# A two-block transformer kernel: the second expert table becomes the stationary operand, and the end of the kernel keeps features on the partitions

## The reference, cut to what matters

```
h = h + peer(rms_norm(h, ffn_norm_gain), w_pq, sub_k1, sub_k2, expert_u, expert_v)
gate = sigmoid(rms_norm(h, ple_norm_gain) @ w_ple_gate)
h = h + gate * (p @ w_ple_proj)

def peer(xn, ...):             # 8 heads; 128 x 128 = 16384 experts
    # top 16 of 128 keys twice per head, top 16 of the 256 pairs -> eidx, gates (128 per token)
    act = gelu(einsum('tkd,td->tk', expert_u[eidx], xn))
    return einsum('tk,tkd->td', act * gates, expert_v[eidx])
```

## Time and profile before

| | us |
|---|---|
| median of 3 runs | 3196.07 |
| the profiled execution | 3203.04 |
| its span | 3201.3 |
| TensorE busy in it | 3064.3 (96%) |
| TensorE weight loads | 2653.1 (83%) |
| VectorE busy | 1886.7 (59%) |
| ScalarE busy | 1458.6 (46%) |
| DMA | 665.24 MB, mean 208 GB/s |

### The profile page before, as it was taken

One profiled execution on the slowest core, in us unless ns is written; L12 is line 12 of the kernel. 1 busy time (PEld: TensorE's weight loads), 2 busy tenths in 40 slices (PEclk: granted clock), 3 DMA queues, 4 the chain that ended last, 5 costly groups with the idle time before them and its releaser, 6 DMA issues. The chain is left out here.

```text
span 3201.3 us, 39991 instructions
## 1 busy us (share of the span) xinstructions
PE 3064.3 (96%) x15672; PEld 2653.1 (83%) x15672; DVE 1886.7 (59%) x2657; ACT 1458.6 (46%) x2137; POOL 159.9 (5%) x282
## 2 busy tenths in 40 slices
PE   8997689999998999999999999999999999999998
PEld 7996677888887887977789899889998888888876
DVE  4445355444444545464558987998755655655554
ACT  4333444444443444354444466347644444444443
POOL 2002100000000000140000100110000000000000
PEclk9996699999999999999999999999999999999999
DMA  7552045555554554545567888888787666777653
GB/s 247 188 188 68 0 148 172 192 185 194 185 188 158 192 196 145 173 142 178 192 211 247 281 304 305 293 278 294 257 276 241 240 231 242 242 248 248 216 194 131
DMA packets 219049, 665.24 MB, mean 208 GB/s; under 512 B 11705, under 2 KB 87513, under 8 KB 169488
## 3 DMA queue, kind: packets, MB, share of 16 engines
q1 hardware_dynamic: 208592, 607.36, 56.6%
q0 software_dynamic: 5440, 35.80, 3.2%
q10 hardware_dynamic: 4864, 19.99, 1.7%
HBM read 623.25 MB, written 37.77 MB: 206 GB/s over the span
## 5 line engine op out<-in xcount | busy, mean ns | idle before, releaser
L195 DVE TENSOR_TENSOR weights_lo<-weights,weights_hi 128x1024 fp32r<-128x1024 f32 (+4 forms) x1080 | 1227.5, 1178 | 974.8 <-ACT weights_hi L188 973.3
L188 ACT ACTIVATE weights_hi<-weights 128x1024 fp32r<-128x1024 f32 (+4 forms) x1080 | 1046.8, 1018 | 1508.8 <-PE banks L444 1121.4
L2185 PE MATMUL banks<-peer_features,weights_hi 128*128 128x448 f32 (+1 forms) x2304 | 743.7, 378 | 18.7 <-DVE weights_lo L195 18.6
L442 PE MATMUL banks<-weights_hi,features_hi 128*128 128x512 f32 (+3 forms) x1728 | 651.5, 377 | 11.4 <-DVE weights_lo L195 11.3
L444 PE MATMUL banks<-weights_hi,features_lo 128*128 128x512 f32 (+3 forms) x1728 | 649.3, 376 | 0.0
L443 PE MATMUL banks<-weights_lo,features_hi 128*128 128x512 f32 (+3 forms) x1728 | 649.1, 376 | 0.0
L2186 PE MATMUL banks<-peer_features,weights_lo 128*128 128x224 f32 (+1 forms) x2304 | 615.1, 267 | 0.0
L2185 PEld LDWEIGHTS banks<-peer_features,weights_hi 128*128 128x128 f32 x2304 | 431.9, 187 | 68.7 <-DVE weights_lo L195 27.9
L2186 PEld LDWEIGHTS banks<-peer_features,weights_lo 128*128 128x128 f32 x2304 | 438.6, 190 | 0.0
L442 PE MATMUL banks<-weights_hi,applied_hi 128*128 128x512 f32 x1024 | 398.5, 389 | 1.1 <-DVE peer_scores L2362 1.1
L444 PE MATMUL banks<-weights_hi,applied_lo 128*128 128x512 f32 x1024 | 398.4, 389 | 0.0
(11 more groups left out here) (377 smaller groups left out, 2101.8 us busy)
## 6 DMA issues: line engine op xcount, KB each, us to landing
weights<-in_expert_u SPq DMA_DIRECT2D x128, 1024.0 KB, 5.8
weights<-in_expert_v SPq DMA_DIRECT2D x128, 1024.0 KB, 5.0
weights<-in_w_ffn_gate SPq DMA_DIRECT2D x44, 1024.0 KB, 5.2
weights<-in_w_ffn_up SPq DMA_DIRECT2D x44, 1024.0 KB, 5.2
weights<-in_w_ffn_down SPq DMA_DIRECT2D x44, 1024.0 KB, 5.0
weights<-in_w_in SPq DMA_DIRECT2D x48, 900.0 KB, 4.7
weights<-in_w_out SPq DMA_DIRECT2D x32, 1024.0 KB, 5.2
weights<-in_w_in SPq DMA_DIRECT2D x24, 704.0 KB, 4.4
```

What stands on the lines that cost most here:

```text
L188: act.activation(hi[:, k, n], raw[:, k, n], ACT.Copy).then_inc(self.hi_ready, 1 + skip)
L195: last = dve.tensor_tensor(lo[:, k, n], raw[:, k, n], hi[:, k, n].bitcast(F32), ALU.subtract)
L442: pe.matmul(out, xh, wh, start=first, stop=False)
L2185: pe.matmul(self.bank(n % 3, 2 * (T - lo)), wh[:, k, :], F[:, k, :, lo:T], start=(k == 0), stop=False)
```

## The change

It has five parts.

1. **Second table.** The stationary operand is now a 128 x 128 tile of the table, and the moving one the weights of 224 tokens: 48 matmuls of 224 columns to a step in place of 24 of 512. The sum lies in PSUM with features on the partitions. At the first step eight matmuls of a zero tile with 512 columns clear the banks.
2. **The 32 tokens.** Their chosen rows of `expert_v` are gathered too, 32 more gathers of 1 MB; VectorE sums them, each scaled, at 64 places (`ADD`) in steps 158 to 261, and 16 small fp32 matmuls with a 0/1 matrix at step 266 add them into the banks. The gate matrix is no longer built for them: steps 126 to 129 of `HOT` and a set of transposes are gone. Scores and gates in DRAM are 224 tokens wide.
3. **The first table's row products** (`SUM`) move from steps 34 to 118 to steps 56 to 73 and 108 to 153, one at each step.
4. **The residual** is turned in place to features on the partitions: 8 times 4 transposes at steps 76, 79, ..., 97 (`BACK`), each with one ScalarE copy of 512 elements.
5. **The end** is part of the same block and the same ring: 16 further steps with `w_ple_gate_2` as the stationary operand, 768 matmuls of 256 columns. The transposes after the second table are gone; norm statistics, sigmoid, product, sum and store (10 stores of 128 or 256 KB) work on features by tokens. `project` in the earlier stage makes the projection in that layout (the same columns in twice as many matmuls). The output is stored transposed, and the host turns it.

```diff
@@ project (earlier stage)
-                for t in range(NT):
+                for m in range(4):
                     for k in range(2):
-                        last = pe.matmul(self.bank(banks + t), pT[:, k, tok(t)], wproj[c // 2][:, c % 2, k, :],
-                                         start=(k == 0), stop=(k == 1))
+                        last = pe.matmul(self.bank(banks + m // 2, T, m % 2 * T), wproj[c // 2][:, c % 2, k, m * P:(m + 1) * P],
+                                         pT[:, k, :], start=(k == 0), stop=(k == 1))
@@ constants of peer
-        SC, RET, TURN = 18, (22, 74), (55, 107, 122)
...
+        SC, RET, TURN = 18, (22, 74), (55, 107)
         ROWS, BUFS = 32, 3
-        HOT = [(58 + i, 0, ROWS // 8 + i) for i in range(16 - ROWS // 8)] + [(110 + i, 1, i) for i in range(16)]\
-            + [(126 + i, 0, i) for i in range(ROWS // 8)]
-        SUM = [34 + 4 * k // 3 for k in range(2 * ROWS)]
+        HOT = [(58 + i, 0, ROWS // 8 + i) for i in range(16 - ROWS // 8)] + [(110 + i, 1, i) for i in range(16)]
+        SUM = [56, 57, *range(58, 74), *range(108, 154)]
         DOTS = SUM[-1] + 1
+        free = [s for s in range(DOTS + 4, 262) if s % 8 != 2]
+        ADD = [free[k * len(free) // (2 * ROWS)] for k in range(2 * ROWS)]
+        GATHERED, BACK = NKEYS - 6, [76 + 3 * j for j in range(KD // 2)]
@@ tensor, first table
+                        if n in BACK:
+                            j = BACK.index(n)
+                            pe.wait_ge(choice_read, 1)
+                            if j > 0:
+                                pe.wait_ge(*x_back(j))
+                            for i in range(2):
+                                for t in range(NT):
+                                    last = pe.transpose(self.bank(5, P, i * T + t * P), chunk(t, 2 * j + i), self.ident[:, :])
+                            last.then_inc(self.turned.sem, 1)
@@ tensor, second table
+                        if e == GATHERED:
+                            pe.wait_ge(row_summed, 4 * ROWS)
+                            for c in range(KD):
+                                pe.matmul(self.bank(c // 2, ROWS, c % 2 * T), row_sum[:, c * P:(c + 1) * P], sel[:, :],
+                                          start=False, stop=False)
                         wh, wl = ring.hi[:, half, :], ring.lo[:, half, :]
-                        for t in ((1, 0) if e == 0 else (0, 1)):
...
-                            for c in range(4):
-                                cols, tok = slice(c * BANK, (c + 1) * BANK), slice(t * P, (t + 1) * P)
-                                last = self.passes(pe, self.bank(4 * t + c), a_hi[:, q % 2, e % 2, tok], a_lo[:, q % 2, e % 2, tok],
-                                                   wh[:, cols], wl[:, cols], e == 0, e == NKEYS - 1)
...
+                        gh, gl = a_hi[:, q % 2, e % 2, :], a_lo[:, q % 2, e % 2, :]
+                        for c in (range(KD) if e > 0 else [*range(6, KD), *range(6)]):
...
+                            out, cols = self.bank(c // 2, DENSE, c % 2 * T + ROWS), slice(c * P, (c + 1) * P)
+                            if e == 0 and c % 2 == 0:
+                                pe.matmul(self.bank(c // 2), zero[:, :], wh[:, 0:BANK], start=True, stop=False)
+                            pe.matmul(out, wh[:, cols], gh, start=False, stop=False)
+                            pe.matmul(out, wl[:, cols], gh, start=False, stop=False)
+                            last = pe.matmul(out, wh[:, cols], gl, start=False, stop=(e == NKEYS - 1 and c % 2 == 1))
+                            if e == NKEYS - 1 and c % 2 == 1 and c < KD - 1:
                                 last.then_inc(applied, 1)
@@ tensor, the 16 steps of the end
+                    for s in range(KD):
+                        b, piece = s // 4, s % 4
...
+                        ring.wait(pe, i, j, half)
...
+                        for c in range(4):
+                            if piece == 0 and b < 2:
+                                pe.wait_ge(added, 4 * b + c + 1)
+                            if piece == 0 and b >= 2:
+                                pe.wait_ge(gate_left, 2 * (b - 2) + c // 2 + 1)
+                            for k in range(4):
+                                kk = 4 * piece + k
+                                if b == c == 0 and k % 2 == 0:
+                                    pe.wait_ge(*f_lo(kk // 2 + 1))
+                                out, cols = self.bank(4 * (b % 2) + c, T), slice(c * P, (c + 1) * P)
+                                pe.matmul(out, wh[:, k, cols], F[:, kk, 0, :], start=(kk == 0), stop=False)
+                                pe.matmul(out, wl[:, k, cols], F[:, kk, 0, :], start=False, stop=False)
+                                last = pe.matmul(out, wh[:, k, cols], F[:, kk, 1, :], start=False, stop=(kk == KD - 1))
@@ vector, gathered rows of the second table
+                            if c == 0:
+                                last = dve.tensor_scalar(to, row, weight, None, ALU.mult)
+                            else:
+                                last = dve.scalar_tensor_tensor(out=to, in0=row, scalar=weight, in1=to, op0=ALU.mult, op1=ALU.add)
+                            last.then_inc(row_summed, 1)
@@ vector, the end: add(j), feature_lo(j), scale(n), out(n)
+                        dve.tensor_tensor(XT[:, j], self.bank(j).rearrange("p (i t) -> p i t", t=T), XT[:, j], ALU.add)\
+                            .then_inc(added, 1)
...
+                        dve.tensor_tensor(gate_of(n), gate_banks(b, c, w), R[:, :].unsqueeze(1).to_broadcast([P, w, T]),
+                                          ALU.mult).then_inc(gate_left, 1)
...
+                        ch(dve.tensor_tensor(gate_of(n), gate_of(n), proj[:, 4 * b + c:4 * b + c + w, :], ALU.mult))
+                        dve.tensor_tensor(chunks(b, c, w), chunks(b, c, w), gate_of(n), ALU.add).then_inc(out_ready, 1)
```

More of the change, by code:

```diff
@@ L2160, in _ @@
                     self.rstd_of_tiles(pool, D)
-                    for c in range(ROWS):
-                        if c % 8 == 0:
+                    for c in range(2 * ROWS):
+                        if c % 8 == 0 and c < ROWS:
                             pool.wait_ge(listed, c // 8 + 1)
@@ L2190, in _ @@
                             for t in range(NT):
-                                last = pe.matmul(self.bank(3, P, t * P), self.ones[:, :], S[:, 0, 0, t * P:(t + 1) * P],
+                                last = pe.matmul(self.bank(3, P, t * P), self.ones[:, :], S_flat[:, t * P:(t + 1) * P],
                                                  start=True, stop=True)
@@ L2247, in _ @@
                                 last.then_inc(applied, 1)
                         last.then_inc(ring.used, 1)
+                    for s in range(KD):
+                        b, piece = s // 4, s % 4
+                        i, j, half = at(END + s)
+                        ring.wait(pe, i, j, half)
+                        wh, wl = [ring.piece(w, half, ple_tiles) for w in (ring.hi, ring.lo)]
+                        for c in range(4):
[11 more added lines that the diff above has]
+                                last = pe.matmul(out, wh[:, k, cols], F[:, kk, 1, :], start=False, stop=(kk == KD - 1))
+                            if b == 3 and piece == 3 and c < 3:
+                                last.then_inc(applied, 1)
+                        last.then_inc(ring.used, 1)
+                        if s == ROWSUM:
+                            pe.wait_ge(*x_squared(KD // 2 + 1))
+                            for t in range(NT):
+                                last = pe.matmul(self.bank(0, 1, T + t), total[:, 0, t * P:(t + 1) * P], self.ones[:, 0:1],
+                                                 start=True, stop=True)
+                            last.then_inc(self.squares.sem, 1)
+                        if s == SPREAD:
+                            pe.wait_ge(diag, 2)
+                            for t in range(NT):
+                                last = pe.matmul(self.bank(1, P, T + t * P), self.ones[:, :], diagonal[:, t * P:(t + 1) * P],
+                                                 start=True, stop=True)
+                            last.then_inc(spread, 1)
@@ new lines, in feature_lo @@
+                    def feature_lo(j):
+                        dve.wait_ge(*f_hi(j + 1))
+                        for i in range(2):
+                            hi, lo = [f[:, 2 * j + i, :] for f in F_ple]
+                            last = dve.scalar_tensor_tensor(out=lo, in0=XT[:, j, i], scalar=ple_gains[2 * j + i],
+                                                            in1=hi.bitcast(F32), op0=ALU.mult, op1=ALU.subtract)
+                        last.then_inc(self.turned_read["dve"].sem, 1)
@@ L2463, in peer @@
+                    for n in range(6, len(groups)):
+                        scale(n)
+                        if n > 6:
+                            out(n - 1)
+                    out(len(groups) - 1)
```

(1 more changed line is left out.)

333 lines of the change are left out of this document (210 added, 123 removed).

## The result

The kernel after takes 3149.34 us (median of 4 runs, 3149.23 to 3149.43), beside 3198.65 for the kernel before on the same chip (4 runs, 3193.03 to 3201.77): ratio 0.9848, 95% interval 0.9831 to 0.9865, so faster by 1.5%. The forecast was 3145 with 3112 to 3175 around it. In five more runs on another chip the ratio was 0.9845 (0.9832 to 0.9859). The profiled execution took 3149.38, its span is 3147.6 where it was 3201.3: 53.7 us less.

A forecast was written before the change was run, and what follows sets the result against it. The matmuls themselves were taken as the bound, with TensorE stalls behind VectorE in two first-table stretches; −10 − 31 − 9 + 8.5 − 9.5 = −51 us from a median of 3196.07 gave 3145, range 3112 to 3175.

The forecast's parts named there:

- The five terms of the sum: Second table −10, first table −31, gap before the gate product −9, gate product +8.5, after its last matmul −9.5 us.
- the +1 for late products at steps 133 and 146: First table: at these steps L2418 meets a row product, which was to cost 1 us.
- 687.3: Second table's forecast length in us: 682.0 for its matmuls, 1.8 for clearing, 3.5 for 16 fp32 matmuls; 696.4 before.
- The gap: Between the second table's last matmul and the gate product's first: 1 us in place of 10.2, −9 us.
- the low end of my two and not the middle: Gate product's price per 256-column matmul: low end 0.1201 us, high end 0.1266, middle 0.1233 taken, giving 94.7 us.
- the fixed 0.0134 taken from 512: Time in us a matmul carries beside its columns: 512 columns at 2.4 GHz are 0.2133 of the 0.2267 measured.
- the remainder of a pair of unlike matmuls: Gate product's high end: a pair of 512 and 256 columns, 0.3533 us, less 0.2267 leaves 0.1266 for 256 columns.
- The tail's chain: After the last matmul: scaling, sigmoid, product, sum over 256 elements, then a store; 5 us in place of 14.5, −9.5.
- the 3.9 worked out: VectorE's work in us beside the second table in one step of 5.3 us, taken as covered.
- R1: Steps 126 to 143: moved work stalls its new place through DMA limits, +12 us, time 3157 to 3165; chance 0.12.
- R2: Second table: the load hides, a 224-column matmul costs 0.1067 us or less, time 3119; chance 0.13.
- R3: Second table: handover comes on top of the load, 0.1266 us a matmul, +86 us, whole kernel 3241; chance 0.06.

The follow-up runs named there:

- the run with short products: Kernel before, each of the first table's 64 row products 128 elements wide instead of 1024, place and order unchanged: 3171.5 us, ratio 0.9916.

## Why the prediction was right

The bound was read rightly. The five terms of the sum all have the sign forecast, and all but one are within some 2 us of their size; that one, and the size of the stall inside another, came from rows that were misread. The median came out 4 us above the forecast: the change gave 49.3 us instead of 51, and the median of before was 3198.65 where the forecast started from 3196.07.

*Parts 2 to 4, first table, −31 against −31.5: the mechanism is right, the closeness is partly luck.* The prediction counted 23 and 32 tiles in the two stretches, put the loss at 32 us and took 29 of it back. The stall was 26 (the run with short products). The count is of whole tiles that VectorE finished, and a tile is 5 us. The matmuls of the same two stretches of the kernel before, 1755 to 1884 and 1978 to 2157, give parts of tiles too:

```profile
L2185 PE MATMUL banks<-peer_features,weights_hi 128*128 128x448 f32 x377 | 120.7, 377 | 7.2 <-DVE weights_lo L195 7.2
...
L2185 PE MATMUL banks<-peer_features,weights_hi 128*128 128x448 f32 x527 | 168.6, 377 | 9.2 <-DVE weights_lo L195 9.2
```

377 and 527 pairs at 0.3133 are 118.1 and 165.1 us, so 10.9 + 13.9 = 25 us were lost there, and 26 over steps 34 to 107. By steps the rest is this: −7.1 over steps 126 to 143, where four one-hot steps are gone (448 records of these matmuls where there were 512; not tried alone); −1.2 over steps 108 to 125, of which 0.5 is a wait of L2228 on L2330; −1.1 for a wait of L442 on L2362 ahead of the second table, which the forecast had set down to part 1; and +3.5 for the transposes of the residual (+4.0 by the run without them). With the −25.9 that is −31.8. So 3 us too many for the stall were made good by small terms that the sum did not have here, and by the +1 for late products at steps 133 and 146, which did not come: there is no wait of TensorE there.

*Part 1, second table, −10 against −4.6: the mis-sized term.* The mechanism was right, a load of 128 columns as the floor, and is now shown from both sides: 687.96 us with 128 columns, 688.00 with 224, and 0.1186 a matmul with 256. Two sizes were off. The pace is 0.1117, not 0.111: 6144 × 0.0007 = 4.3 us, and 0.001 us in such a price is 6. The price was in the trace, and its reading was off. The prediction divided the whole length of a row by its matmuls. The loads of the same L787 in the kernel before, from the middle of the run on:

```profile
381.51 3.32 PEld L787 LDWEIGHTS banks<-sgu_v,sgu_w_turned 128*128 128x128 f32 x29
```

A load of them is recorded with 0.19, so they are (3.32 − 0.19) / 28 = 0.1118 apart. The first distance between matmuls of that run is 0.06, since the first load lay ahead of it, and pulls the mean down to the 0.110 that was read. The 16 transposes do stand 0.109 apart in steady state; 0.111 was a value between the two. And 1.6 us are the half clock behind the 16 narrow matmuls, which I had priced at 3.5 (3.6 measured) with nothing behind them. 4.3 + 1.6 is what parts 687.3 from 693.2.

The Trainium skill, "TensorE: Matmul & The Clock Gate", section "LDWEIGHTS (loading the stationary operand)", gives a load's columns over 1.2 GHz, an estimate of 106.7 ns for 128. The distance measured with 128 and with 224 columns is 5 ns over that in each matmul, 31 us in this kernel. Measurement decides: 0.1117.

*Part 5.* The gap is gone altogether (−10.2 for −9), since TensorE's wait on the first feature pair is 0.2 us. The gate product takes 93.6 us, of which 768 matmuls at 0.120 are 92.2: the low end of my two and not the middle (in the long stream of the second table 256 columns even take 0.1186). So the columns at 2.4 GHz plus the fixed 0.0134 taken from 512 was the right model here, and the remainder of a pair of unlike matmuls was not. The tail's chain is short as forecast. VectorE in order of time at the end of the kernel after, then its stores:

```profile
3143.50 0.42 DVE L2617 TENSOR_TENSOR peer_scratch<-banks,peer_rstd 128x256 f32<-128x256 f32 x1 [0.22 <-PE banks L2323]
...
3145.08 0.42 DVE L2624 TENSOR_TENSOR residual<-residual,peer_scratch 128x256 f32<-128x256 f32 x1
```

```profile
out<-residual SPq DMA_DIRECT2D x6, 256.0 KB, 6.4
...
out<-residual SPq DMA_DIRECT2D x4, 128.0 KB, 1.7
```

*VectorE beside the second table.* The groups of VectorE in 2370 to 3050 us, kernel after:

```profile
L195 DVE TENSOR_TENSOR weights_lo<-weights,weights_hi 128x1024 fp32r<-128x1024 f32 x252 | 297.4, 1222 | 196.5 <-ACT weights_hi L188 196.5
L2554 DVE SCALAR_TENSOR_TENSOR row_tokens<-expert_rows,row_gates,row_tokens 128x1024 f32<-128x1024 f32 x62 | 79.3, 1279 | 0.0
L2588 DVE TENSOR_TENSOR applied_lo<-normed,applied_hi 128x448 fp32r<-128x448 f32 x62 | 38.4, 619 | 3.4 <-ACT applied_hi L2437 3.4
L2560 DVE TENSOR_TENSOR normed<-normed,peer_rstd 128x1792 f32<-128x1792 f32 x15 | 30.3, 2018 | 0.0
```

A sum takes 1.28 us, not 1.22, a split of 448 elements 0.62, not 0.60; and VectorE is busy for 171.15 of 240 us, 71% of a step of 5.36, or 3.8 us against the 3.9 worked out. Idle time behind L188, 196.5 us, is the cover that was left.

*R1* asked for 337 GB/s where 309 had been seen. The stretch 2260 to 2356 moves 369 GB/s at a DMA share of 0.97, with TensorE at 96.00 of 96. 309 was what had been asked, not what could be had. The gathers did land later, 9.9 us in the median instead of 6.4:

```profile
expert_rows<-in_expert_rows,attention_statistics POOLq DMA_INDIRECT x32, 9.9
expert_rows<-in_expert_v,attention_statistics POOLq DMA_INDIRECT x32, 7.7
```

but within the 20 us that three buffers give. *R2* fell, since the pace is 0.1117 and not 0.1067 or less, and *R3* since nothing comes on top of the load. R3 was to decide from 0.1194 a matmul; 256 columns come close to it (0.1186, and the whole kernel then at 0.9983 of before).

What stays open: which of the 16 matmuls' properties takes the clock down (their 32 columns or their data type, fp32 and not fp32r), and why the clock came back after 3 us behind 224 columns and not within 60 behind 128.

## What to carry to other kernels

Which operand to keep stationary is settled by what is the longer, the columns moved or the 128-column load: here 0.1117 us a matmul is the floor, between 128 and 224 columns nothing is added, and 256 already cost 6% more. So the other operand's size should be brought just under the crossing and the rest done elsewhere, as 32 tokens were. A price that is multiplied by thousands is best taken from a long stream of the same form; where there are only short runs, it is read between neighbours in the middle of the run, not as the mean of a whole row. A loss is read from the work done in a stretch in its smallest unit, not from whole tiles. And work that fills an engine beside the bound is best moved to where that engine idles: moving half of it gave back half of the stall.

## What the hardware showed that was not expected

- Fewer columns made the kernel slower: 3180 us with 128, 3149 with 224. Both run at the same pace while the clock is full, but once it had fallen, behind 16 matmuls of 32 columns, it stayed at 0.50 for over 60 us with 128 columns and for about 3 us with 224.
- The floor follows the granted clock. At 0.50, matmuls of 128 columns behind a 128-column load stand 60 / 283 = 0.212 us apart, against 0.1117 at full clock: it doubles but for about 0.01 us. In the kernel after, the matmuls of 224 columns behind the narrow ones stand as far apart, eleven distances in 3018.60 − 3016.25 = 2.35 us or 0.214 each, where 224 columns at 1.2 GHz are 0.187: there too it is not the columns that set the pace.
- One core moved 369 GB/s for 96 us while TensorE never waited.
